# When ScalarE copies head 3's plain query rows in the first step of the first block's attention

## What is computed

```python
def mla_attention(q_lat, kv_lat, k_rope_raw, cos, sin, q_norm_g, w_uq, kv_norm_g, w_ukv):
    q = (rms_norm(q_lat, q_norm_g) @ w_uq).reshape(B, S, N_HEADS, QK_NOPE + QK_ROPE)
    q_nope, q_pe = q[..., :QK_NOPE], apply_rope(q[..., QK_NOPE:], cos, sin)
    kv = (rms_norm(kv_lat, kv_norm_g) @ w_ukv).reshape(B, S, N_HEADS, QK_NOPE + V_HEAD)
    ...
    for start in range(0, S, Q_BLOCK):
        s = (jnp.einsum("bqhd,bkhd->bhqk", q_nope[:, start:end], k_nope[:, :end])
             + jnp.einsum("bqhd,bkd->bhqk", q_pe[:, start:end], k_pe[:, :end]))
        ...
        p = jax.nn.softmax(jnp.where(causal, s, NEG_INF), axis=-1).astype(v.dtype)
        outs.append(jnp.einsum("bhqk,bkhd->bqhd", p, v[:, :end]))

def mixer_sublayer(...):
    ...
    merged = jax.nn.sigmoid(gate_a) * y_rnn + jax.nn.sigmoid(gate_b) * y_mla
    return merged @ w_out
```

## Time and profile before

| | us |
|---|---|
| three timed runs: median (lowest to highest) | 2770.6 (2770.31 to 2772.05) |
| the profiled execution | 2761.56 |
| its span, first to last instruction | 2759.7 |
| TensorE busy | 2692.1 |
| ScalarE busy | 1100.0 |
| mean granted clock of TensorE | 0.986 of full |

### The profile page before, as it was taken

How to read it: one execution, slowest core, us unless ns; L and a number is a source line. 1 busy time by engine, 2 the same in 40 slices (tenths; PEclk the granted TensorE clock), 3 DMA queues, 4 the chain that set the end, 5 groups by cost and what they waited for, 6 DMA issues and landing times. The chain is left out here.

```text
span 2759.7 us, 35281 instructions
## 1 busy us (share of the span) xinstructions
PE 2692.1 (98%) x12370; PEld 2103.2 (76%) x12370; DVE 1726.4 (63%) x2512; ACT 1100.0 (40%) x1901; POOL 1602.9 (58%) x985
## 2 busy tenths in 40 slices
PE   8999999999999999999999999999999999999998
PEld 6777778888887777778888877778777677787775
DVE  6787755444126777654443138876777678777775
ACT  3733424222025543432221031554555515545554
POOL 5754466666676744486666765577236564772263
PEclk9999999999999999999999979999999999999999
DMA  4322222233332322223333323236797232257951
GB/s 155 91 70 69 62 84 84 92 99 99 92 92 84 100 62 65 66 79 97 99 97 94 108 67 98 71 97 227 287 355 239 69 92 77 92 209 279 352 189 65
DMA packets 89530, 338.21 MB, mean 123 GB/s; under 512 B 21552, under 2 KB 24368, under 8 KB 80048
## 3 DMA queue, kind: packets, MB, share of 16 engines
q1 hardware_dynamic: 66592, 298.02, 32.6%
q0 software_dynamic: 19008, 26.28, 3.7%
q10 hardware_dynamic: 3792, 12.06, 1.2%
HBM read 366.67 MB, written 33.55 MB: 145 GB/s over the span
## 5 line engine op out<-in xcount | busy, mean ns | idle before, releaser
L184 POOL TENSOR_TENSOR wl<-ring,wh 128x1024 fp32r<-128x1024 f32 x317 | 780.6, 2463 | 26.4
L182 POOL TENSOR_SCALAR wh<-ring 128x1024 fp32r<-128x1024 f32 x317 | 353.5, 1115 | 730.4 <-PE ps L261 516.0
L259 PE MATMUL ps<-xh,wh 128*128 128x512 f32 x1592 | 634.3, 398 | 20.9 <-DVE xl L1272 11.9
L261 PE MATMUL ps<-xh,wl 128*128 128x512 f32 x1592 | 621.9, 391 | 0.0
L260 PE MATMUL ps<-xl,wh 128*128 128x512 f32 x1592 | 621.6, 390 | 0.0
L259 PEld LDWEIGHTS ps<-xh,wh 128*128 128x128 f32 x1592 | 299.9, 188 | 102.3 <-issue 12.6
L261 PEld LDWEIGHTS ps<-xh,wl 128*128 128x128 f32 x1592 | 299.8, 188 | 63.8
L260 PEld LDWEIGHTS ps<-xl,wh 128*128 128x128 f32 x1592 | 300.2, 189 | 60.9 <-issue 1.0
L1519 DVE SCALAR_TENSOR_TENSOR taps<-ps,par,taps 128x511 f32<-128x511 f32 x192 | 143.9, 749 | 231.8 <-ACT taps L1246 216.9
L3118 DVE TENSOR_TENSOR ew_l<-ew,ew_h 128x1024 fp32r<-128x1024 f32 x184 | 213.8, 1219 | 6.0 <-ACT ew_h L2641 5.9
L2641 ACT ACTIVATE ew_h<-ew 128x1024 fp32r<-128x1024 f32 x184 | 180.5, 1051 | 11.2 <-DMA ew<-in_eu 8.5
(11 more groups left out here) (556 smaller groups left out, 5310.5 us busy)
## 6 DMA issues: line engine op xcount, KB each, us to landing
ring<-in_w SPq DMA_DIRECT2D x343, 512.0 KB, 3.6
ew<-in_eu SPq DMA_DIRECT2D x32, 2048.0 KB, 12.3
ew<-in_ed SPq DMA_DIRECT2D x32, 1024.0 KB, 11.3
xrows<-xr ACTq DMA_DIRECT2D x8, 512.0 KB, 2.7
yrows<-xr ACTq DMA_DIRECT2D x8, 512.0 KB, 3.6
yg<-yrows SPq DMA_DIRECT2D x8, 512.0 KB, 5.3
z<-in_x SPq DMA_DIRECT2D x4, 512.0 KB, 5.7
out<-z SPq DMA_DIRECT2D x8, 256.0 KB, 2.9
```

Of the source, the lines that this page charges most:

```text
L182: nc.gpsimd.tensor_scalar(hi, raw, 1.0, 0.0, ALU.mult, ALU.add).then_inc(sem["w_hi"], 1)
L184: nc.gpsimd.tensor_tensor(lo, raw, hi, ALU.subtract).then_inc(sem["w_split"], 1)
L259: nc.tensor.matmul(out, wh, xh, start=first, stop=False, **kw)
L261: return nc.tensor.matmul(out, wl, xh, start=False, stop=last, **kw)
```

## The change

ScalarE's `evac_q(3)` moves from behind `expo(1)`, inside the loop, to ahead of the loop, right behind the key copies. A wait for all eight score pieces of heads 0 and 1 goes with it, since the copy overwrites the half of `qt` that `scores(1)` reads. Both layers run this code.

```diff
                     gelu(7)
                     evac_q(2)
                     evac_k(1)
+                    act.wait_ge(sem["s_mm"], at("s_mm", 8))
+                    evac_q(3)
                     act.wait_ge(sem["rnn_done"], at("rnn_done", PAIRS))
                     evac_pt(0)
                     for p in range(PAIRS):
...
                         expo(h + 1)
                         if p:
                             evac_pt(h)
-                        else:
-                            evac_q(3)
                         if more:
                             expo(h + 2)
```

## The result

| | before | changed |
|---|---|---|
| timed runs, median | 2770.45 us (6 runs) | 2755.26 us (6 runs) |
| lowest to highest | 2765.7 to 2772.05 | 2753.57 to 2757.29 |
| the profiled execution | 2761.56 | 2753.57 |
| its span | 2759.7 | 2751.8 |

The ratio is 0.9949, 95% interval 0.9939 to 0.996: 15.2 us shorter. The two profiled executions differ by 7.99 us only. So the question of this study is where the rest of the 15.2 us is.

What follows compares the result with a forecast made beforehand. TensorE, busy 98% of the span, was taken as the bound, waiting for ScalarE's late query copy. Savings of 5.29 us (layer 0) and 3.55 us (layer 1), 8.84 together, from 2770.60 gave 2761.8 us; range 2757 to 2768.

Steps and rivals of the forecast that it cites:

- The waits and the place of the copy: First gate half, both layers: the early copy fits ScalarE's idle time at no cost; turn 5.29 and 3.55 us earlier.
- What is late next: Before head 1's turn: VectorE's rotation keeps some 0.6 us of slack a layer, and nothing takes the gain back.
- The wait moves to the rotation: Rival, before turn(1): stretched normalisation delays the rotation, 1.7 us wait a layer, 3.4 us given back, 2765.2 us; chance 0.11.
- The clock: Behind the idle times at the first gate half: half clock costs 1.61 us in layer 0, nothing in layer 1.
- The clock pays twice: Rival: timed runs may lose clock behind both layers' idle times; saving 10.45 us, 2760.2 us; chance 0.14.
- No gain: Rival: something else holds TensorE at the same place, or the step loses the time again; 2770.6 us; chance 0.08.
- the column sums: Rival, the block's four norms: shifted sums meet half clock, losing 2.7 us a norm, 10.9 in all; 2772.7 us; chance 0.04.

Runs made afterwards that it cites:

- four: The changed kernel with four more 64 x 512 ScalarE copies ahead of the moved evac_q(3); ratio 0.9962 against the kernel before.
- same: The kernel before, unchanged, timed once more beside itself; ratio 0.9997.
- after: The profiled execution of the changed kernel from the first measurement; 2753.57 us.
- again: The changed kernel, unaltered, timed once more in a later set; ratio 0.9954 against the kernel before.
- layer0: The kernel before with the copy moved early in layer 0 only; ratio 0.9978 against the kernel before.
- fill7: The kernel before, copy still late, with 7 extra unread matmuls in the idle time of layers 0 and 1; ratio 0.9992 against the kernel before.

## Why the prediction was wrong

**The waits and the place of the copy: right.** The forecast had the copy end near 172.5, 0.5 us before its successor could start; it was 0.54. It had the exponentials unmoved, the first gate half 0.23 us behind the rope projection, and the turn 5.29 and 3.55 us earlier; measured in the two profiled executions it was 5.42 and 3.69, as from the first gate half to the turn it took 7.64 us in place of 7.77. Without the clock the two idle times are worth 178.52 - 174.84 = 3.68 and 983.30 - 979.76 = 3.54 us, 7.2 together; the table's rest gives 7.0 +- 0.5.

**What is late next: right for the rotation's slack, wrong in what stands behind it.** 0.6 us of slack was forecast and 0.40 us measured, with no wait. But the first thing that binds if ScalarE is late is the exponentials ahead of head 2's scores, as four showed. The rival *The wait moves to the rotation* did not come true. Its condition, a longer division, did not either: 2.00 us.

**The clock: this step failed.** The sum has 1.61 us of clock, read from one execution, with the sentence "so this execution has no clock to win there". That was true of the execution and was used for the median of the timed runs. Of seven executions six lost clock in layer 1, 1.3 to 2.8 us, and the mean of both places is 3.2 us, twice the term. The rival *The clock pays twice* had this right in mechanism and in size: its 2 x 1.61 us are the 3.2 measured, though a single place lost anything from 0 to 2.8. But the 2760.2 us of that rival are still 4.9 above the measured median, so this term is not the whole of the miss. From 8.84 to 15.2 us it is 6.4 us. Of these 2.0 lie at the two steps, which are worth 10.8 us and not 8.84, and 1.6 of the 2.0 are this clock. Another 2.6 us are clock that no trace places, and 1.8 us are what the first sample showed beyond the mean of all runs. The range ended at 2757, which left hardly any room for such a time.

**The 9.0 us that were passed over.** The prediction noted that the median of the timed runs stood 9.0 us above the profiled execution, and took the saving over from the one to the other as it was. That was a sign. Executions of this kernel differ by their clock (same), so a profiled execution at the short end has lost less clock than the others, and a clock term read from it is suspect. It did not say where. The five other whole traces of the kernel before have 91 us at half clock on average and the first has 77; of the 15 us between them 5.4 lie behind the two idle times and 10.2 between 2190 and 2540 us; the other places add and take about the same. The Trainium skill (TensorE: Matmul & The Clock Gate, Why this matters for your kernels) has an idle gap between bursts of matmuls bring the lower clock back. The first trace agreed in one layer of two; of the fourteen idle times seen by now eleven agree.

**No gain, and the column sums.** The first is refuted by all timed runs of the change. The second happened in small. In both traces of the changed kernel, `after` and `again`, the clock fell during the first norm's sums, earlier against them than before, and stayed at half for 10.2 us around this norm, where all six whole traces of the kernel before have 6.8:

```profile
400.60:404.40 3.80, 3.59 (x30) 0.94 0.33 130
```

This line counts 30 of the 32 matmuls; the last two start after 404.40. From the first to the last they took 4.1 us (400.7 to 404.8), where it was 3.6 with 1.00 throughout before. `four`, with the same early copy, has the 10.2 us too, and `layer0`, which is the changed kernel up to there, has 6.8; so it was not chance of one execution, and is not certain either. The lead of the changed kernel shrank from 5.9 us ahead of this norm (400.7 against 406.6) to 5.1 at layer 1's rope projection (974.42 against 979.53), a fraction of what that rival asked for.

## What to carry to other kernels

Where TensorE sets the pace, an idle time can cost its length and clock behind it: here 3.5 us of idle time and, in eleven cases of fourteen, 1.3 to 2.8 us more. Read the second part from several executions, since one can show none of it. When the timed runs lie well above the profiled execution, look first at the mean clock of each run: a clock term read from a favourable trace is too small. And before a small gain is explained to the last us, take the kernel before often enough: six runs of it left 1.8 us of this gain to their sample. And a copy that only frees a buffer should stand where its engine is idle, even ahead of work that was issued for an earlier head, if what it waits for is there by then.

## What the runs showed of the hardware

- Executions of one and the same kernel on one chip spread over 17 us (2761.89 to 2779.25), and their mean granted clock goes along, from 0.986 to 0.980. That is 0.6%, of single executions.
- Behind the same idle time of 3.4 to 3.5 us TensorE ran at full clock in three of fourteen cases, in six 3.4 us and in five 6.8 us at half clock. The stretches of 3.4 us cost 1.3 to 1.6 us of time, those of 6.8 us 2.6 to 2.8. An idle time of 1.9 us was followed by such a stretch in one of the two cases of fill7's trace.
- Extra matmuls whose result nobody reads, in two idle times, made the kernel 5.7 us shorter (ratio 0.9979, 0.9968 to 0.9989).
- In layer 0 of the changed kernel VectorE's division of a head (four instructions) took 1.27 us with 0.14 us beside GpSimd's splitting, 2.00 us with 0.92 us beside it, and 4.26 us where both started together (188.24 and 188.25) in the first profile of the kernel before.
